# Seven block products instead of eight in the first matrix of two gated feed-forward layers, and the second matrix in four passes between them

## The reference, cut to what matters

```
D_FF = 2816
def conv_ffn(h, g_norm, w_in, conv_w, conv_b, w_out):
    L = h.shape[1]
    xn = rms_norm_2(h, g_norm)
    a, b = jnp.split(xn @ w_in, 2, axis=-1)
    ap = jnp.pad(a, ((0, 0), (CONV_W - 1, 0), (0, 0)))
    a_conv = conv_b
    for j in range(CONV_W):
        a_conv = a_conv + ap[:, j:j + L] * conv_w[j]
    return h + (jax.nn.silu(a_conv) * b) @ w_out
```

## Time and profile before

| what | value |
|---|---|
| median of three runs | 3136.31 us |
| span of the profiled execution | 3134.2 us |
| first matrix, layer 1, main stretch | 249.62 us for 2040 matmuls (2112 in all) |
| second matrix, layer 1 | 128.47 us |
| first matrix, layer 2, main stretch | 241.09 us for 1530 matmuls (1584 in all) |
| second matrix, layer 2 | 122.85 us |

### The profile page before, as it was taken

The page is one execution under the profiler, slowest core; times in us unless marked ns, Lnnn a source line. Parts: engine busy times, 40 slices in busy tenths (PEclk is TensorE's granted clock), DMA queues, the critical chain, the costliest instruction groups (busy, mean ns, idle before and its releaser), DMA issues.

```text
span 3134.2 us, 47541 instructions
## 1 busy us (share of the span) xinstructions
PE 2990.2 (95%) x17673; PEld 2612.4 (83%) x17673; DVE 2025.2 (65%) x3238; ACT 1261.6 (40%) x2075; POOL 1157.7 (37%) x564
## 2 busy tenths in 40 slices
PE   6999999998999999999999999899999998999998
PEld 3766679998988888888887788699999975799986
DVE  4767515999977778788886255466651375466622
ACT  3347333446963333333333334432222446432221
POOL 2420333664014444455553222044444430244442
PEclk9998999999999999999999999799999999999999
DMA  6710223555679999999996211023223420122231
GB/s 247 280 60 1 62 93 96 166 175 191 227 248 350 346 328 341 337 351 350 346 347 229 75 55 41 14 88 94 87 88 101 117 81 1 41 89 93 94 101 67
DMA packets 179876, 509.22 MB, mean 162 GB/s; under 512 B 14881, under 2 KB 72353, under 8 KB 175393
## 3 DMA queue, kind: packets, MB, share of 16 engines
q1 hardware_dynamic: 72288, 262.57, 25.4%
q0 software_dynamic: 37440, 136.40, 11.9%
q10 hardware_dynamic: 70016, 108.54, 10.3%
HBM read 467.60 MB, written 39.85 MB: 162 GB/s over the span
## 4 chain that ended last, share of the span: by engine, by line
PE 87%; ACT 5%; DVE 4%; issue 2%; DMA 1%; ACTq 0%; DVEq 0%
PE ps L1279 23%; PE ps L1230 17%; PE ps L1167 16%; PE ps L1533 8%; PE ps L901 8%; ACT arena L1960 2%; PE ps L1351 2%; PE ps L952 1%; ACT arena L1976 1%; PE ps L1680 1%; PE ps L1299 1%; PE ps L1457 1%; PE ps L1414 1%; PE ps L654 1%; PE ps L1421 1%
## 5 line engine op out<-in xcount | busy, mean ns | idle before, releaser
L2314 POOL TENSOR_TENSOR w_lo<-ring,w_hi 128x1024 fp32r<-128x1024 f32 x300 | 755.0, 2520 | 1387.9 <-ACT w_hi L795 1387.8
L795 ACT ACTIVATE w_hi<-ring 128x1024 fp32r<-128x1024 f32 x500 | 525.4, 1055 | 771.9 <-PE ps L1230 277.4
L1230 PE MATMUL ps<-w_hi,arena_r 128*128 128x512 f32 x1536 | 426.8, 397 | 4.5 <-DVE arena_r L2772 4.5
L1167 PE MATMUL ps<-h_hi,w_hi 128*128 128x384 f32 x1024 | 355.5, 347 | 5.0 <-issue 5.0
L1230 PEld LDWEIGHTS ps<-w_hi,arena_r 128*128 128x128 f32 x1536 | 289.0, 189 | 72.2 <-DVE arena_r L2772 5.0
L1167 PE MATMUL ps<-h_lo,w_hi 128*128 128x384 f32 x1024 | 348.9, 341 | 0.0
L1279 PE MATMUL ps<-h_hi,w_hi 128*128 128x264 f32 (+2 forms) x1536 | 347.5, 298 | 0.6 <-DVE arena L2869 0.5
L1167 PE MATMUL ps<-h_hi,w_lo 128*128 128x384 f32 x1024 | 346.4, 338 | 0.0
L1279 PE MATMUL ps<-h_lo,w_hi 128*128 128x264 f32 (+2 forms) x1536 | 346.2, 297 | 0.0
L1279 PE MATMUL ps<-h_hi,w_lo 128*128 128x264 f32 (+2 forms) x1536 | 345.6, 297 | 0.0
L2327 POOL DMA_INDIRECT arena<-u_rows,arena x128 | 193.4, 1511 | 375.8 <-DVE arena L2748 354.5
(11 more groups left out here) (343 smaller groups left out, 5444.0 us busy)
## 6 DMA issues: line engine op xcount, KB each, us to landing
ring<-weight_stream SPq DMA_DIRECT2D x500, 512.0 KB, 3.7
gates<-arena ACTq DMA_DIRECT2D x12, 2048.0 KB, 7.3
arena<-gates ACTq DMA_DIRECT2D x32, 768.0 KB, 14.3
arena<-w_modulation ACTq DMA_DIRECT2D x17, 1024.0 KB, 5.3
early_acts<-arena ACTq DMA_DIRECT2D x64, 192.0 KB, 2.7
arena<-early_acts ACTq DMA_DIRECT2D x32, 384.0 KB, 7.7
arena<-w_modulation ACTq DMA_DIRECT2D x2, 2560.0 KB, 15.0
x<-x_t ACTq DMA_DIRECT2D x1, 2112.0 KB, 19.5
```

The costliest lines, as they stand in the source:

```text
L795: act.activation(w_hi[:, s, :], ring[:, s, :], ACT.Copy).then_inc(hi_ready, 1)
L1167: last = pe.matmul(ps[:, bank, 0:ND], w, v, start=c == 0 and p == 0, stop=c == DC - 1 and p == 2)
L1230: last = pe.matmul(ps[:, Y_BANKS[b][half], :], a[u], w[v][:, half * BANK:(half + 1) * BANK], start=first and p == 0, stop=final and p == 2)
L2314: pool.tensor_tensor(w_lo[:, s, :], ring[:, s, :], w_hi[:, s, :], ALU.subtract)\
```

## The change

For each tile `f` the two products `a` and `b` are taken as one product of 2 x 2 blocks: the weights have two column blocks (gate, other) and two row blocks (even and odd chunks of the 1024 features), the tokens two halves. Instead of eight block products there are seven (Strassen's scheme in Winograd's form): A11, A22, S1, A12, S2, S4, S3, each 4 chunks x 3 matmuls of 264 (258 in layer 2) columns, so 84 matmuls a round in place of 96, or of 48 and 24 wide ones.

- **Sums of tokens.** Once per layer, while the attention's output projection runs, ACT and DVE make the differences and sums of halves (`ffn_t1`, `ffn_w`) and their high and low parts (`t_hi`, `t_lo`). Odd chunks need three more combinations each.
- **Sums of weights.** In every round DVE makes four sums of half slots (`weight_sum`, 128 x 512).
- **Halves.** ACT and POOL work on half slots (128 x 512), eight of them ahead of PE. A round has seven of them in place of four halves' worth (two whole slots).
- **Joining.** ACT copies four partial results a round out of PSUM (`keep_product`), PE goes on adding in the same bank once the copy is made; DVE adds them up (`join_a`, `join_b`). The first tap moves from DVE to ACT (`first_tap`).
- **Second matrix.** It is cut in four passes over 6, 6, 6 and 4 tiles `f`. Its blocks (units "out", four blocks of 128 x 128 each, half a slot) stand between the products of the first matrix: none in rounds 0 to 5, two a round in rounds 6 to 17, three in 18 to 20, one in 21, and the last ten behind. `x` gets 32 additions a layer in place of 8. The padding is gone: 22 slots, not 24. Most of them come from a tensor of their own, `ffn_out`, into buffers outside the ring.
- The loops over `f` are unrolled. Outside the feed-forward layers some semaphores are merged, with other counts; the work is the same.

```diff
+FFN_PARTS = (6, 6, 6, 4)
+PRODUCTS = ("A11", "A22", "S1", "A12", "S2", "S4", "S3")
+SUMS = ("S1", "S2", "S4", "S3")
+KEPT = ("A11", "S1", "S2", "S3")
+def ffn_units():
+    units, out = [], 0
+    for f in range(FC):
+        units += [("A11", f)] + ([("A22", f - 1)] if f else []) + [("S1", f), ("A12", f), ("S2", f)]
+        between, behind = (0, 0) if f < 6 else (1, 1) if f < 18 else (2, 1) if f < FC - 1 else (0, 1)
+        for _ in range(between):
+            units.append(("out", out))
+            out += 1
+        units += [("S4", f), ("S3", f)]
+        for _ in range(behind):
+            units.append(("out", out))
+            out += 1
...
 PE
+                    w = half_of(w_hi, m), half_of(w_lo, m)
+                    for j in range(DC // 2):
+                        ready(j)
+                        for p, (u, v) in enumerate(three(src(j), (w[0][:, j * P:(j + 1) * P], w[1][:, j * P:(j + 1) * P]))):
+                            last = pe.matmul(ps[:, bank, 0:width], u, v, start=start and j == 0 and p == 0,
...
 POOL
+            def half_lows(k):
+                for m in range(NUNITS):
+                    pool.wait_ge(hi_ready, unit0(k) + m + 1)
+                    pool.tensor_tensor(half_of(w_lo, m), raw_half(k, m), half_of(w_hi, m), ALU.subtract).then_inc(lo_ready, 1)
...
 DVE, a round
+                for f in range(FC):
+                    if f:
+                        gate(f - 1)
+                    if f + 1 < FC:
+                        weight_sum(k, "S4", f + 1)
+                        weight_sum(k, "S3", f + 1)
+                    join_a(f, 0)
+                    if f:
+                        low_gated(f - 1)
+                    for p, t in outs_within(UNIT["S2", f], UNIT["S4", f]):
+                        add_out(p, t)
+                    join_a(f, 1)
+                    norm_a(f)
+                    if f + 2 < FC:
+                        weight_sum(k, "S1", f + 2)
+                        weight_sum(k, "S2", f + 2)
+                    taps(f)
+                    join_b(f)
```

More of the change, by code:

```diff
@@ L377, in build @@
         MID = (HALO + L) // 2
[L378 to L391, removed]
+        FFN_HALVES = (((0, HALF), (HALF, L)), ((HALO, MID), (MID, L)))
@@ new lines, in out_unit, with outs_within, out_banks, out_tokens @@
+        def out_unit(p, t):
+            n = FFN_PARTS[p]
+            return UNIT["out", p * PASS_UNITS + (t * n + n - 1) // 4]
+        def outs_within(first, end):
+            return [(p, t) for p in range(len(FFN_PARTS)) for t in range(DC) if first <= out_unit(p, t) < end]
+        def out_banks(k, p, t):
+            return ps[:, 2 * (t % 2), 0:L - META] if k else ps[:, 2 * (t % 2):2 * (t % 2) + 2, 0:HALF]
+        def out_tokens(k, a):
+            return a[:, META:L] if k else a.rearrange("p (a b) -> p a b", a=2)
@@ L888, in _ @@
+            load_turns(1, TURN["ffn0"])
+            load_ffn(0)
+            for s in range(RING):
+                sp.wait_ge(lo_ready, unit0(0) + released(2 * FC + s))
+                sp.dma_start(ring[:, s, :], stream[MLA_TURN * RING + s]).then_inc(slot_loaded[s], 16)
+            load_turns(MLA_TURN + 1, TURN["ffn1"])
+            load_ffn(1)
         @block.tensor
@@ L1271, in _, with part2 @@
                 last.then_inc(y_made, 1)
[L1274 removed]
+            def part2(s, c, pair, src=(h_hi, h_lo), spans=((0, HALF), (HALF, L))):
                 h = src[0][:, c, :], src[1][:, c, :]
@@ L1281, in part2, with tile2 @@
                 return last
-            def tile2(name, turn, s, pair, src=(h_hi, h_lo), spans=FFN_SPANS[0][0], between=None):
+            def tile2(name, turn, s, pair, src=(h_hi, h_lo), spans=((0, HALF), (HALF, L)), between=None):
                 split_wait(pe, name, turn, s)
@@ new lines, in ffn, with tokens, product @@
+                width = halves[0][1] - halves[0][0]
+                U0, C0, F0 = unit0(k), k * len(KEPT) * FC, k * FC
+                def tokens(c, half):
+                    lo, hi = halves[half]
+                    return h_hi[:, c, lo:hi], h_lo[:, c, lo:hi]
+                def product(m, bank, src, ready, start, stop):
+                    w = half_of(w_hi, m), half_of(w_lo, m)
[3 more added lines that the diff above has]
+                            last = pe.matmul(ps[:, bank, 0:width], u, v, start=start and j == 0 and p == 0,
+                                             stop=stop and j == DC // 2 - 1 and p == 2, skip_group_check=True)
+                    last.then_inc(slot_used, 1)
```

611 lines of the change are left out of this document (448 added, 163 removed).

## The result

| kernel | median us | lowest to highest | runs | ratio to before, 95% interval |
|---|---|---|---|---|
| before | 3136.16 | 3134.22 to 3138.06 | 4 | |
| changed | 3195.66 | 3191.14 to 3197.44 | 4 | 1.0190 [1.0176, 1.0205] |

A forecast was written before the change was run, and what follows sets the result against it. It took TensorE's unbroken matmuls as the bound, DVE and POOL in rounds without records. Layer 1: -32.3 + 18.5 + 5 = -8.8; layer 2: -27.8 + 18.5 + 5 = -4.3; together -13 us, forecast 3123 us, range 3085 to 3165.

The forecast's parts named there:

- shelter of 2.4 us: Rounds with records: DVE's PSUM instructions, additions included, and the SiLU wait hide 2.4 us of the 8.1 us of meetings.
- Matmuls removed, -60.1 us: Both layers' first product: fewer matmuls save 32.3 us in layer 1 and 27.8 in layer 2, if nothing waits.
- Rival (d): Matmuls on TensorE: changing weights show, so the product does not get cheaper as forecast; 3146 us, chance 0.05.
- Rounds 1 to 5: Rounds without second-matrix units (records): DVE and POOL bind them at 14.0 us against TensorE's 10.3, +18.5 us a layer.
- shelter of 1.6 us: Rounds without records: DVE's three PSUM instructions and the SiLU wait hide 1.6 us of the 6.3 us of meetings.
- price of the seven meetings: Rounds without records: each POOL half slot costs DVE 0.9 us, seven cost 6.3 us.
- Rounds 6 to 17, zero with a margin of 0.2 us: Rounds with two second-matrix units (records): TensorE binds at 16.1 us (15.7 in layer 2), DVE with meetings 15.9; no loss.
- rival (b): Rounds with records are bound by DVE and POOL too, about 17.0 us each; 3155 us, chance 0.27.
- Ring loads, zero: Weight transfers into the ring: places are released about 6 us before the sum needing them; no added wait.
- Start, 3 us a layer: Layer start: S2 needs all combined tokens, some 6 us with hand-overs against 4.4 of cover; 3 us (0 to 6).
- End, 2 us a layer: Layer end: gated tile 21's path, then one addition due every 2.9 us where it was 16; 2 us (0 to 4).
- To the letter: Rounds without records under the skill page's full blocking: 15.8 us, adding 18 us to the sum; the forecast followed the trace.

The follow-up runs named there:

- run 1: Changed kernel, but GpSimd makes the low part of only 64 of the 512 columns of each weight half, leaving out part of the computation: span 3112.1 us.
- run 4: Run 3's kernel, with VectorE making 504 of 512 columns of the low parts of the four sum halves (S1 to S4) instead of GpSimd: 3158.8 us, ratio 1.0059.
- run 2: Changed kernel, with SyncE issuing the ring load of slot 39 ahead of the load of out unit 13: span 3183.0 us.
- run 5: Run 3's kernel, with the second record unit of round 18 (out unit 25) moved behind product S3(18): span 3170.8 us.
- run 3: Changed kernel with run 2's edit, additions ahead of low parts at a layer's end, and merged sum and root behind A12(0) at its start: 3183.3 us, ratio 1.0152.
- run 7: Run 6's kernel, with VectorE making 504 of 512 columns of the low parts of all seven product halves: span 3131.3 us.
- run 8: Run 7's kernel, with the low parts of A22(f) and A11(f+1) ahead of the sums in rounds without records: 3133.22 us, ratio 0.9996.
- run 6: Run 4's kernel with run 5's shift, and the low parts of S4 and S3 one round earlier in rounds without records: 3142.48 us, ratio 1.0022.

## Why the prediction was wrong

Four of its steps failed. It took the rounds with records as bound by TensorE, with a shelter of 2.4 us that does not exist: they cost 15 us. It priced waits on ring loads at zero: 10 us. It priced the start of a layer at 3 us and measured 11, and the end at 2 us and measured 20 in layer 1. The mechanism, that DVE and POOL exclude each other and bind the rounds without records, was right. Point by point:

- **Matmuls removed, -60.1 us**: right. Where nothing waits (run 1) a round takes 10.2 and 10.1 us for the forecast's 10.3 and 10.1, and rounds with records 16.07 and 15.71 for 16.1 and 15.7. Rival (d) falls.
- **Rounds 1 to 5**: the mechanism was right (DVE and POOL exclude each other, TensorE falls 4.5 us a round behind its need, PSUM rows untouched). The size was near by luck, since two errors half cancel: 14.81 and 14.68 us for 14.0 and 13.8, some 7 us over the eight whole steps. The fifth step of each layer already has a unit of the second matrix in it and cost 1.6 and 1.8 us where the forecast had 3.7, 4 us less in all, so 3 us are left. Three terms were off. DVE's own work is 8.1 us, not 9.3, since the lengths of rows that follow each other overlap by about 0.08 us. The shelter of 1.6 us did not exist: in the timeline's steady state each half slot of POOL catches one two-operand SBUF instruction, seven of seven. And 0.3 us of waits stay. The price of the seven meetings was right, 6.4 us for 6.3.
- **Rounds 6 to 17, zero with a margin of 0.2 us, "the weak spot"**: wrong. 16.63 and 16.55 us, +6 and +9 us over the eleven steps: rival (b), which said 17.0 here and 14.7 without records. Its numbers don't follow from its rule, though. The rows that read PSUM are 1.3 us, 2.2 with the additions; with only these as shelter it comes to 15.6 - 1.3 = 14.3 and 18.3 - 2.2 = 16.1. What the runs show is no shelter at all, on a smaller own time. Nine meetings at 0.92 with 8.1 + 0.8 of DVE's own give 17.2; steps of 17.3, 16.4 and 16.1 alternate, the last at TensorE's own need. Run 1 (16.07) and run 4 (16.08) show, in layer 1, that it is POOL's time.
- **Ring loads, zero**: wrong by 9.7 us (4.4 and 5.3 at the steps 17 to 18). I checked when the ring place is released, not what stands in SP's queue ahead of its load. Runs 2 and 5 show two waits one behind the other there, the queue's and the gated tile's.
- **Start, 3 us a layer**: 11.0 and 10.8. I priced the path of the tokens, not that the first sums, ACT's roundings and POOL's first halves fall into the same microseconds. Run 1 took 8.7 and 8.2 us off it; run 3, which moved only the root, 0.5 and 0.1. So it is mostly the exclusion again. The output projections in front of it took 1.4 and 1.3 us more.
- **End, 2 us a layer**: 2.8 in layer 2, about 20 in layer 1: 8.7 of waits, 3.1 at the lower clock behind them, and 7.6 from TensorE's last matmul to the last addition. There one addition is due every 2.9 us, and between two of them DVE waits for ACT's high part, and makes a low part that may meet a POOL instruction of 2.4 us. The forecast had seen that the additions come closer and had not asked what stands between them in DVE's program. Run 3 took 14.5 us off, 5.3 of which came back behind it. Run 1, with POOL's half slots short, left this end at 55.2; its whole slots stood there as before, so what they cost at this place was not measured alone.

Together: -13 + 3 + 15 + 10 + 16 + 3 + 19 = +53, and 5 us ahead of, between and behind the layers, in lines that the change does not touch: 58 by this account, 57.2 with the decimals kept, for 60.8 measured. The 3 to 4 us between them are not assigned. The part ahead of the layers, 4.3 us in the two profiles, may be scatter: over the executions shown here the first addition to `x` ended between 2033.96 and 2048.33 us, also in kernels that are alike up to it. What sets that is open.

The Trainium skill, page "SBUF — State Buffer", says in its Terms that the loser of the port pair fully blocks. The rows agree that the two exclude each other, but not for the whole instruction: a half slot that takes POOL 1.29 us alone lengthened DVE by 0.64 to 1.1 us, 0.92 on average, close to the 0.9 of the forecast; in full it would have been 9.0 us in seven meetings, not 6.4. To the letter a round was to take 15.8 us; it took 14.8.

What stays open: I did not try a kernel that keeps the changed order of work and avoids only the meetings. Nor one that reads the second operand of the sums from PSUM, or one with shorter sums. I did not separate the start of a layer further. What run 1 shows holds for POOL's time and its collisions together, since it shortens both; runs 4, 7 and 8, which give DVE more to do and still shorten the round, tell that the collisions count.

## What to carry to other kernels

When TensorE's work is cut by a few per cent, add up DVE's own time and the number of GpSimd's instructions times the price of a meeting, with no shelter, for each kind of round, before counting any gain: here 8.1 + 7 x 0.92 was over TensorE's 10.3, and rounds forecast at zero with a margin of 0.2 us cost 15 us, more than the whole forecast gain. Take an instruction's price from start to start of a run of them, not from its length. For each queue and each place where something falls due more often than before, write down what stands in front of it there; a stall removed shows the next one, and a wait may have sheltered a meeting.

## What I had not expected of the hardware

- Meetings fall in step. With work queued on both sides every half slot of POOL meets exactly one SBUF instruction of DVE, round after round: the steps are 14.79 to 14.83 us in layer 1.
- A half slot costs less on DVE (0.59 us from start to start) than on POOL (1.29 us alone, 0.92 us on DVE as a meeting). Moving seven of them onto the busier engine, together with the new orders of runs 3 to 8, shortened the round from 14.8 to 12.2 us.
- In run 8 POOL's 8 columns read about 0.5 us and passed beside DVE's rows without stretching them. Part of that is probably time held up, since 64 columns read 0.32 us in run 1 while DVE was idle.

```profile
2121.28 0.51 POOL L2662 TENSOR_TENSOR w_lo<-arena,w_hi 128x8 fp32r<-128x8 f32 x1 [3.33 <-DVE w_lo L3336]
2121.87 0.51 POOL L2662 TENSOR_TENSOR w_lo<-ring,w_hi 128x8 fp32r<-128x8 f32 x1
```

- The granted clock fell with the waits, between its two levels of 1.2 and 2.4 GHz: on average 0.93 in rounds 1 to 5 of the changed kernel, where TensorE sat idle 3 us a round, and 0.77 in the window at the end of layer 1 that holds its wait of 5.5 us; in rounds 1 to 5 of layer 1 in run 1, where it never waited, 1.00. In a round the waits are 3.0 us of the 4.5 that TensorE falls behind, and most of the rest is matmuls at the lower level: behind a wait of 2.81 us they start 0.22 us apart instead of 0.122. It cost the rounds nothing, since DVE's rows there show no wait for TensorE; at the end of the layer it made two units 4.7 us long instead of 3.2.
